# Mixture-of-experts slots: one expert for each slot of 128 pairs, and the last norm's factor put on after the gate product

## The chip, the cores and the metric

The kernel runs on one core of one Trainium2 chip. The metric is the time of one execution on the device, in microseconds (us). Engines are named PE (TensorE, matmul), DVE (VectorE), ACT (ScalarE), POOL (GpSimd) and SP (SyncE, which here only issues transfers).

## The reference, cut to what matters

Two transformer blocks follow each other on 512 tokens of width 1024. The change lies at the end of the first: a mixture of 16 experts in 4 groups, and a gated embedding behind it.

```python
def hierarchical_moe(h, ...):        # top-1 group, then top-2 experts inside it
    a = jnp.einsum('td,edf->tef', ht, w_gate)      # 16 experts, 1024 -> 256
    u = jnp.einsum('td,edf->tef', ht, w_up)
    hid = jax.nn.silu(a) * u * combine[..., None]  # combine is 0 for 14 of 16 experts
    out = jnp.einsum('tef,efd->td', hid, w_down)   # 256 -> 1024

x = x + hierarchical_moe(rms_norm(x, ffn_norm_g), ...)
h3 = rms_norm(x, ple_norm_g)
x = x + jax.nn.sigmoid(h3 @ w_pg) * (p @ w_ple)
```

Only two experts count for a token: 1024 pairs of token and expert.

## The kernel before, in words

**Precision.** Every float32 operand of a large product is split in two float32r parts: ACT copies it (hi), DVE or POOL subtracts (lo), and PE makes three matmuls (hi by hi, lo by hi, hi by lo). For weights this is `split_hi` and `split_lo` (L382, L386); a weight slot is 128 x 2048, 1 MB.

**Routing** (`route_tensor`, `route_scalar`, `route_vector`, L1406 to L1559). DVE finds group and experts with small operations that wait for each other. Tokens are sorted by group into 7 slots of 128 rows (4 groups, 3 spare slots, `SLOTS`). POOL scatters the rows into `sorted_h` in HBM and loads a slot's rows into `hg` (L1641, L1647); the first slot's tokens are permuted by 64 small matmuls (L1437) and are split by ACT (L1789) and DVE (L1833).

**Steps** (`moe_*`, L1601 to L1866). A slot is worked on by all four experts of its group: 28 steps (`STEPS`). A step has three weight units of 1 MB (`unit_in` twice, `unit_down` once), 36 matmuls of 512 columns: 24 for gate and up (`gate_up`, L1729 to L1731), 12 for down (`down`, L1757 to L1759), and two turns of the hidden rows (L1740). Units live in four buffers in turn: SP issues unit u's load once unit u-4 is split (L1608), in order of u; ACT makes hi (L1694) once it has landed and PE has used unit u-4; then DVE makes lo (L1699). `POOL_UNITS` gives the down unit of every second step to POOL. DVE's order in step n is: `hid` (L1848), the down unit's split if it is DVE's, unit 3n+5, `g_lo` (L1853), tokens of the next slot if due, unit 3n+6. PE's order is gate_up(n, 0), turn of hidden n-1, turn of the next slot's tokens (L1711, one step in four), gate_up(n, 1), down(n-1). The four experts add up in PSUM; every fourth step ACT copies the sum to `y_sb` (L1795) and POOL stores it (L1661).

**Behind the steps.** POOL waits for all stores and gathers the rows back into `y_back` (L1675), PE turns them (L1782), DVE adds them to `x` (L1862) and the squares to `ss`, PE sums these (L462), ACT makes `rstd`, DVE and ACT make the normed and split h (L478, L488, L495), and only then does PE begin the gate product with `w_pg`, four slots of 48 matmuls (`ple_*`). The second block's context is turned (L1879) and normed (L1895, L1965 to L1986) between them.

**Other places.** POOL writes zeros over `sorted_h` at the start of the kernel (L1141).

## Time and profile before

| | us |
|---|---|
| median of 3 runs | 1744.39 |
| lowest, highest | 1741.7, 1758.29 |
| the profiled execution | 1744.98 |
| its span | 1743.2 |
| granted clock of the span | 0.985 |

Times in rows are us from the span's start. In a row of the timeline the second number is the length; the bracket holds the idle time before and what ended it. In a group by line the numbers behind the bar are the busy us, the mean ns of one, and the idle time before with what ended it. A row of windows has the length, then the busy us (and count) of PE, PE's weight loads, DVE, ACT and POOL, then the granted clock (1.00 is 2.4 GHz, 0.50 is 1.2 GHz), the busy share of the DMA engines and GB/s.

### The profile page before, as it was taken

To read this page: it belongs to the slowest core of one execution; us is meant where nothing else is said; L and a number is where in the kernel's file an instruction comes from. 1 tells how busy PE (TensorE), PEld (TensorE's weight loads), DVE (VectorE), ACT (ScalarE), POOL (GpSimd) and SP (SyncE) were. 2 spreads that over 40 slices of the span, in tenths; PEclk is the share of its full clock that TensorE was granted. 3 is DMA by queue.
4 is the path that set the end of the run, shared out by engine and by line. 5 is a ranking of instruction groups with operands and counts; after the bars stand their busy time and mean duration, and the time that the engine had idled before them with its cause. 6 is when DMAs were issued, how large, how long until landed. Compare 5 with 4: busy or idle time off the path is not lost.

```text
span 1743.2 us, 20038 instructions
## 1 busy us (share of the span) xinstructions
PE 1655.1 (95%) x7715; PEld 1308.7 (75%) x7715; DVE 875.6 (50%) x1010; ACT 775.9 (45%) x901; POOL 125.0 (7%) x87
## 2 busy tenths in 40 slices
PE   6999999999998889859999999999999999999998
PEld 5777777887876777647688888876788688888886
DVE  6434434444577777747642342421355665565464
ACT  5553454223467666727443343351223543443333
POOL 2101101000222223210010000000000000000000
PEclk8999999999999999979999999999999999999999
DMA  7456553223599999931421211131323133333322
GB/s 226 133 188 222 193 179 123 77 82 125 168 342 346 355 330 323 327 139 49 143 68 49 73 57 64 62 110 49 121 87 105 51 97 105 89 96 98 95 79 67
DMA packets 183202, 247.82 MB, mean 142 GB/s; under 512 B 10236, under 2 KB 151000, under 8 KB 179808
## 3 DMA queue, kind: packets, MB, share of 16 engines
q1 hardware_dynamic: 178911, 232.21, 40.4%
q0 software_dynamic: 4224, 14.72, 2.1%
q8 instruction: 43, 0.70, 0.2%
q14 instruction: 24, 0.19, 0.0%
HBM read 233.23 MB, written 13.67 MB: 142 GB/s over the span
## 4 chain that ended last, share of the span: by engine, by line
PE 78%; DVE 9%; DMA 5%; ACT 4%; issue 2%; SPq 1%; POOL 0%; ACTq 0%; DVEq 0%; POOLq 0%
PE psum L409 20%; PE psum L410 19%; PE psum L411 19%; DMA raw_more<-in_w_up 4%; DVE w_lo_more L1699 3%; PE psum L2466 2%; ACT w_hi_more L1694 1%; PE psum L709 1%; DVE w_lo L1699 1%; DVE pre L488 1%; PE psum L792 1%; PE psum L1203 1%; PE psum L1437 1%; PE psum L1204 1%; PE psum L1205 1%
## 5 line engine op out<-in xcount | busy, mean ns | idle before, releaser
L409 PE MATMUL psum<-h_hi,w_hi 128*128 128x512 f32 x1160 | 466.0, 402 | 7.7 <-DVE w_lo L386 3.2
L411 PE MATMUL psum<-h_hi,w_lo 128*128 128x512 f32 x1160 | 453.5, 391 | 0.0
L410 PE MATMUL psum<-h_lo,w_hi 128*128 128x512 f32 x1160 | 453.4, 391 | 0.0
L386 DVE TENSOR_TENSOR w_lo<-raw,w_hi 128x2048 fp32r<-128x2048 f32 (+2 forms) x99 | 223.7, 2259 | 228.4 <-ACT w_hi L382 228.4
L409 PEld LDWEIGHTS psum<-h_hi,w_hi 128*128 128x128 f32 x1160 | 218.4, 188 | 69.4 <-issue 18.4
L411 PEld LDWEIGHTS psum<-h_hi,w_lo 128*128 128x128 f32 x1160 | 218.6, 188 | 46.9
L410 PEld LDWEIGHTS psum<-h_lo,w_hi 128*128 128x128 f32 x1160 | 218.8, 189 | 46.4 <-issue 3.6
L382 ACT ACTIVATE w_hi<-raw 128x2048 fp32r<-128x2048 f32 (+2 forms) x100 | 187.9, 1879 | 75.3 <-PE psum L411 70.0
L1699 DVE TENSOR_TENSOR w_lo_more<-raw_more,w_hi_more 128x2048 fp32r<-128x2048 f32 x41 | 115.0, 2804 | 50.0 <-ACT w_hi_more L1694 50.0
L439 ACT ACTIVATE sq<-x 128x512 f32<-128x512 f32 x56 | 35.4, 632 | 161.0 <-DVE x L1316 105.2
L1694 ACT ACTIVATE w_hi<-raw 128x2048 fp32r<-128x2048 f32 x42 | 80.4, 1914 | 35.7 <-DMA raw<-in_w_up 16.6
L1694 ACT ACTIVATE w_hi_more<-raw_more 128x2048 fp32r<-128x2048 f32 x41 | 78.5, 1914 | 24.0 <-DMA raw_more<-in_w_up 15.7
L1699 DVE TENSOR_TENSOR w_lo<-raw,w_hi 128x2048 fp32r<-128x2048 f32 x29 | 66.2, 2284 | 20.4 <-ACT w_hi L1694 20.4
L1699 POOL TENSOR_TENSOR w_lo<-raw,w_hi 128x2048 fp32r<-128x2048 f32 x13 | 60.7, 4671 | 146.1 <-ACT w_hi L1694 146.1
L409 PE MATMUL psum<-d_hi,w_hi 128*128 128x512 f32 x176 | 69.3, 394 | 0.0
L410 PE MATMUL psum<-d_lo,w_hi 128*128 128x512 f32 x176 | 69.3, 394 | 0.0
L411 PE MATMUL psum<-d_hi,w_lo 128*128 128x512 f32 x176 | 69.3, 394 | 0.0
L2649 ACT ACTIVATE cv<-psum,vec 128x512 f32<-128x512 f32 x44 | 32.0, 777 | 82.3 <-PE psum L411 82.3
L2672 DVE SCALAR_TENSOR_TENSOR cv<-psum,vec,cv 128x511 f32<-128x511 f32 x44 | 32.8, 746 | 52.7 <-ACT cv L2649 52.7
L1316 DVE SCALAR_TENSOR_TENSOR x<-psum,mod,x 128x512 f32<-128x512 f32 x32 | 23.3, 750 | 51.9 <-PE psum L411 51.9
L1729 PE MATMUL psum<-w_hi_more,s_hi 128*128 128x512 f32 x112 | 45.9, 410 | 1.6 <-DVE s_lo L1833 1.6
L1729 PE MATMUL psum<-w_hi,s_hi 128*128 128x512 f32 x112 | 45.1, 403 | 0.0
(380 smaller groups left out, 2595.4 us busy)
## 6 DMA issues: line engine op xcount, KB each, us to landing
raw<-in_w_up SPq DMA_DIRECT2D x72, 512.0 KB, 6.5
wm_raw<-in_w_mod SPq DMA_DIRECT2D x24, 1024.0 KB, 5.9
raw<-in_w_in SPq DMA_DIRECT2D x18, 1024.0 KB
raw<-in_w_in SPq DMA_DIRECT2D x33, 512.0 KB
raw<-in_w_gate SPq DMA_DIRECT2D x28, 512.0 KB, 5.1
raw_more<-in_w_down SPq DMA_DIRECT2D x28, 512.0 KB, 6.2
raw<-in_w_down SPq DMA_DIRECT2D x28, 512.0 KB, 5.9
raw_more<-in_w_gate SPq DMA_DIRECT2D x27, 512.0 KB, 5.0
```

The costliest lines, as they stand in the source:

```text
L382: act.activation(w_hi[j][:, 0:tiles, :], raw[j][:, 0:tiles, :], ACT.Copy).then_inc(G["hi_ready"], 1)
L386: dve.tensor_tensor(w_lo[j][:, 0:tiles, :], raw[j][:, 0:tiles, :], w_hi[j][:, 0:tiles, :].bitcast(F32), ALU.subtract).then_inc(G["lo_ready ...
L409: pe.matmul(to, w_hi[j][:, tile, :], hi_k, start=(k == 0), stop=False)
L410: pe.matmul(to, w_hi[j][:, tile, :], lo_k, start=False, stop=False)
L411: return pe.matmul(to, w_lo[j][:, tile, :], hi_k, start=False, stop=last)
L439: act.activation(sq[:, c % 2, :], x[:, c, :], ACT.Square).then_inc(G["sq_ready"], 1)
L1694: act.activation(u_hi[b][:, :, :], raw_of(u)[:, :, :], ACT.Copy).then_inc(E["e_whi"], 1)
L1699: eng.tensor_tensor(u_lo[b][:, :, :], raw_of(u)[:, :, :], u_hi[b][:, :, :].bitcast(F32), ALU.subtract)\
L1729: pe.matmul(to, t_hi, hi[:, :, k, :], start=(part == 0 and k == 0), stop=False)
L2466: done = pe.matmul(psum[:, 5 + g % 2, :], fd[:, g, i, part * P:(part + 1) * P], dft_l[:, part, i, :], start=(n == 0), stop=(n == 7))
L2649: act.activation(cv[:, s % 2, half, :], psum[:, 2 * ((j0 + s) % 2) + half, :], ACT.Identity, bias=vec[:, bass.ds(V_CONVB + col, 1)], scale ...
L2672: dve.scalar_tensor_tensor(out=buf[:, 1:T], in0=bank[:, 0:T - 1], scalar=vec[:, bass.ds(V_CONV2 + col, 1)], in1=buf[:, 1:T], op0=ALU.mult, ...
```

## The change: what it does, and the diff

Pairs of token and expert take the place of tokens. There are 16 slots, one for each expert, and 7 spare ones: 23 slots, 23 steps, each with one expert's three units. Each step has its own 128 rows, which POOL gathers from `h_rows` by an indirect DMA two steps ahead; PE turns and ACT and DVE split them in every step. After each step DVE (no longer ACT) copies the 128 x 1024 result and POOL stores it by an indirect DMA to `y_rows`; indices beyond the last row are left out of the transfer. The last slot's result is not stored but spread over the tokens by 16 matmuls with a 0/1 matrix (`last_pick`). `POOL_UNITS` now has the down unit of all steps but the last two. Behind the steps four plain DMAs bring two rows for each token (4 MB), DVE adds the two halves, and the gate product with `w_pg` starts at once on h without the norm's factor; DVE multiplies `rstd` on where the product leaves PSUM. The context's norm moves from behind the second slot to behind the third. The zeros at the start are gone. The routing (not shown in full) works on 16 experts: four operations on 128 x 320, about thirty smaller ones, eight 128 x 128 comparisons (`hot`), and 11 + 9 + 8 small matmuls.

```diff
-RC_U, RC_IOTA, RC_TILE, RC_BEFORE, RC_BLOCK, RC_OWN, RC_HIGH, RC_SLOT = 0, P, P + 4, P + 8, P + 24, P + 40, P + 44, P + 48
-RC_COLS = RC_SLOT + EXTRA * (GROUPS - 1)
+NOWHERE = 4096
+
+
...
+            dve.tensor_tensor(g_exp[:, :, :], rt[:, :, 0:GROUPS], wide(g_top[:, :], GROUPS), ALU.subtract)\
...
+            step(dve.tensor_tensor(in_slot[:, :, :], wide(slots, SLOTS), rows(const_row(RC_SLOT, SLOTS), TOP * NT), ALU.is_equal))
+            codes = rc[:, RC_CODE:RC_LEVEL].rearrange("p (n v o) -> p n v o", v=2, o=1).to_broadcast([P, TOP * NT, 2, SLOTS])
+            dve.tensor_tensor(coded[:, :, :, :], in_slot[:, :, :].rearrange("p n (o s) -> p n o s", o=1)
+                              .to_broadcast([P, TOP * NT, 2, SLOTS]), codes, ALU.mult).then_inc(E["e_hot"], 1)
+            places = place[:, :, :].rearrange("p j i -> p (j i)")
+            for m in range(TOP * NT):
+                dve.tensor_scalar(hot[:, m, :], const_row(RC_PLACE, P), places[:, m:m + 1], None, ALU.is_equal)\
+                   .then_inc(E["e_hot"], 1)
+            dve.wait_ge(E["e_matched"], LISTED)
+            listed = psum[:, ROUTE_BANK, LIST0:LIST0 + 2 * SLOTS]
+            dve.tensor_copy(at_row[:, :, :], listed.rearrange("p (v s) -> p v s", v=2)).then_inc(E["e_routed"], 1)
+            step(dve.tensor_copy(last_row[:, :], listed[:, SLOTS - 1:SLOTS]))
 
...
-        POOL_UNITS = [unit_down(n) for n in range(1, STEPS - 1, 2)]
+        POOL_UNITS = [unit_down(n) for n in range(STEPS - 2)]
...
+            def store_tokens():
+                to = h_rows.rearrange("(i p) d -> p i d", p=P)
+                for half in range(2):
+                    sp.wait_ge(G["h_hi_ready"], 8 * N_MOE + 4 * half + 4)
+                    sp.dma_start(to[:, :, half * T:(half + 1) * T], h_tok[:, :, half * T:(half + 1) * T])\
+                      .then_inc(E["e_stored"], 16)
...
+                if n == 0:
+                    store_tokens()
+                else:
                     load_down(n - 1)
...
+                if n == 4:
+                    sp.wait_ge(E["e_matched"], SHARED)
+                    sp.dma_start(tokens[:, :], const["tokens"]).then_inc(E["e_wr"], 16)
+                if n == 8:
+                    sp.wait_ge(E["e_routed"], LAST_PICKED)
                     sp.dma_start(ctx_in[:, :, :], a["ctx_2"].rearrange("(i p) n -> p i n", p=P)).then_inc(L["ctx_in"], 16)
...
         def moe_gpsimd(pool):
-            pool.wait_ge(W["zero_out"], 16 * (SLOTS + 1))
-            pool.wait_ge(G["h_hi_ready"], 8 * N_MOE + 8)
+            pool.wait_ge(G["chunk_done"], 2 * (G_WO + 3) + 2)
+            for j in range(2):
+                pool.memset(hg[j][:, :], 0.0).then_inc(W["wm_silu"], 1)
+
+            def gather(s):
+                if s >= 2:
+                    pool.wait_ge(E["e_turned"], tokens_turned(s - 2))
+                pool.indirect_dma_start(hg[s % 2][:, :], None, h_rows,
+                                        bass.IndirectOffsetOnAxis(ap=at_row[:, 0, s:s + 1], axis=0),
+                                        bounds_check=T - 1, oob_is_err=False).then_inc(E[f"e_hg{s % 2}"], 16)
+
+            def store_y(s):
+                pool.indirect_dma_start(y_rows, bass.IndirectOffsetOnAxis(ap=at_row[:, 1, s:s + 1], axis=0),
+                                        y_sb[:, :], None, bounds_check=PAIRS - 1, oob_is_err=False)\
...
-                pool.indirect_dma_start(sorted_h, bass.IndirectOffsetOnAxis(ap=at_row[:, i:i + 1], axis=0),
...
-            def load_tokens(s):
-                if s >= 3:
...
+            pool.wait_ge(W["wm_silu"], 5)
+            for s in range(2):
+                gather(s)
+            pool.memset(y_sb[:, :], 0.0).then_inc(W["wm_silu"], 1)
...
+            store_y(SLOTS - 1)
             for n in range(STEPS):
...
+                if n + 2 < SLOTS:
+                    gather(n + 2)
+                if n:
+                    pool.wait_ge(E["e_ycopy"], n)
+                    store_y(n - 1)
                 if unit_down(n) in POOL_UNITS:
                     unit_lo(pool, unit_down(n))
...
+            pool.wait_ge(E["e_ystore"], 16 * SLOTS)
+            wait_unit_lo(pool, UNITS - 1)
             pool.wait_ge(E["e_turned"], tokens_turned(SLOTS - 1))
...
+            from_rows = y_rows.rearrange("(j i p) d -> p j i d", j=TOP, p=P)
+            for half in range(2):
+                for j in range(TOP):
+                    pool.dma_start(y_back[:, j, :, half * T:(half + 1) * T], from_rows[:, j, :, half * T:(half + 1) * T])\
+                        .then_inc(E[f"e_hg{half}"], 16)
...
+        def pick_bank(c):
+            return (6, 7, 0, 1)[c % 4]
+
+        BACK_BANKS, LEAD = (2, 3, 4, 5), 2
...
+            def turn_back(c):
+                if c % 4 == 0:
+                    pe.wait_ge(E["e_chain"], ROUTE_STEPS + KC + c // 4 + 1)
+                if c >= 4:
+                    pe.wait_ge(G["x_ready"], 8 * R_MOE + c - 3)
+                for i in range(NT):
+                    done = pe.transpose(psum[:, BACK_BANKS[c % 4], i * P:(i + 1) * P], y_back[:, 0, i, c * P:(c + 1) * P], ident)
+                done.then_inc(L["turned"], 1)
...
+            def first_gate(c):
+                if c == 0:
+                    pe.wait_ge(G["lo_ready"], G_PG + 1)
+                pe.wait_ge(G["h_lo_ready"], 8 * N_PLE + c + 1)
+                for half in range(2):
+                    done = product(pe, psum[:, half, :], 0, of_pairs(half, c), h_hi, h_lo, c, c == KC - 1)
+                    if c == KC - 1:
+                        done.then_inc(G["chunk_done"], 1)
...
             def down(n):
-                s, e, u = n // PER_GROUP, n % PER_GROUP, unit_down(n)
+                u = unit_down(n)
...
-                if e == 0:
-                    if s:
-                        pe.wait_ge(E["e_ycopy"], s)
-                    else:
-                        pe.wait_ge(L["p_done"], 7)
+                if n:
+                    pe.wait_ge(E["e_ycopy"], n)
+                else:
+                    pe.wait_ge(L["p_done"], 7)
...
+            turn_tokens(0)
+            share()
             for n in range(STEPS):
                 gate_up(n, 0)
                 if n:
                     turn_hidden(n - 1)
-                if n % PER_GROUP == 2 and n // PER_GROUP + 1 < SLOTS:
-                    turn_tokens(n // PER_GROUP + 1)
+                if n + 1 < SLOTS:
+                    turn_tokens(n + 1)
                 gate_up(n, 1)
                 if n:
                     down(n - 1)
...
+            pe.wait_ge(E["e_lo"], LAST)
+            pe.wait_ge(E["e_routed"], LAST_PICKED)
...
+            pe.wait_ge(E["e_chain"], ROUTE_STEPS + KC)
+            for c in range(KC + LEAD):
+                if c < KC:
+                    turn_back(c)
+                if c >= LEAD:
+                    first_gate(c - LEAD)
...
             for n in range(STEPS):
                 act.wait_ge(E["e_used"], unit_in(n, 1) + 1)
...
                 unit_hi(act, 3 * n + 4)
-                if n % PER_GROUP == 0 and n:
-                    copy_y(n // PER_GROUP - 1)
                 unit_hi(act, 3 * n + 5)
...
-                if n % PER_GROUP == 1 and n // PER_GROUP + 1 < SLOTS:
-                    tokens_hi(n // PER_GROUP + 1)
+                if n + 2 < SLOTS:
+                    tokens_hi(n + 2)
                 unit_hi(act, 3 * n + 6)
...
+            def copy_y(n):
+                dve.wait_ge(E["e_used"], unit_down(n) + 1)
+                dve.wait_ge(E["e_ystore"], 16 * n + 16)
+                dve.tensor_copy(y_sb[:, :].rearrange("p (b t) -> p b t", b=2), psum[:, Y_BANK:Y_BANK + 2, :])\
+                   .then_inc(E["e_ycopy"], 1)
+
...
                                          in1=act_u[:, n % 2, :], op0=ALU.mult, op1=ALU.mult).then_inc(E["e_hid"], 1)
                 dve_lo(3 * n + 4)
+                if n:
+                    copy_y(n - 1)
                 dve_lo(3 * n + 5)
                 dve.wait_ge(E["e_hi"], hidden_turned(n))
                 dve.tensor_tensor(g_lo[:, n % 2, :, :], psum[:, HID_BANK + n % 2, 0:2 * P].rearrange("p (j t) -> p j t", j=2),
                                   g_hi[:, n % 2, :, :].bitcast(F32), ALU.subtract).then_inc(E["e_lo"], 1)
-                if e == 1 and s + 1 < SLOTS:
-                    tokens_lo(s + 1)
+                if n + 2 < SLOTS:
+                    tokens_lo(n + 2)
...
+            dve.wait_ge(E["e_hi"], LAST)
...
+            for c in range(KC):
+                dve.wait_ge(E["e_turned"], LAST + c)
+                dve.tensor_tensor(x[:, c, :], x[:, c, :], psum[:, pick_bank(c), :], ALU.add).then_inc(E["e_chain"], 1)
+            for s in range(2):
+                split_lo(dve, G_PG + s, (G_PG + s) % 2)
+            for half in range(2):
+                cols = slice(half * T, (half + 1) * T)
+                dve.wait_ge(E[f"e_hg{half}"], 16 * ((SLOTS + 1 - half) // 2 + TOP))
+                dve.tensor_tensor(y_back[:, 0, :, cols], y_back[:, 0, :, cols], y_back[:, 1, :, cols], ALU.add)\
+                   .then_inc(E["e_chain"], 1)
+            dve.wait_ge(E["e_chain"], ROUTE_STEPS + KC)
...
             for c in range(KC):
                 dve.wait_ge(L["turned"], c + 2)
-                dve.tensor_tensor(x[:, c, :], x[:, c, :], psum[:, c % 4, :], ALU.add).then_inc(G["x_ready"], 1)
+                dve.tensor_tensor(x[:, c, :], x[:, c, :], psum[:, BACK_BANKS[c % 4], :], ALU.add).then_inc(G["x_ready"], 1)
                 if c:
-                    add_square(dve, R_MOE, c - 1, N_MOE + 1)
-            add_square(dve, R_MOE, KC - 1, N_MOE + 1)
+                    gained_lo(c - 1)
+            gained_lo(KC - 1)
+            for c in range(KC):
+                add_square(dve, R_MOE, c, N_MOE + 1)
...
+            for k in range(KC):
+                if k == 4:
+                    norm_mean(pe, N_PLE)
+                    for n in range(2):
+                        turn_context(n)
+                for half in range(2):
+                    done = product(pe, psum[:, 2 + half, :], 1, of_pairs(half, k), h_hi, h_lo, k, k == KC - 1)
+                    if k == KC - 1:
+                        done.then_inc(G["chunk_done"], 1)
             pe.wait_ge(L["ctx_copied"], 2)
             for n in range(2, 4):
...
+                for i in range(2):
+                    c = 2 * s + i
+                    dve.wait_ge(G["chunk_done"], 2 * (G_PG + s) + i + 1)
+                    if c >= 2:
+                        dve.wait_ge(L["pg_sig"], c - 1)
+                    dve.tensor_tensor(pre[:, i, :], psum[:, 2 * ((G_PG + s) % 2) + i, :], rstd[:, :], ALU.mult)\
+                       .then_inc(G["pre_ready"], 1)
...
+                if s == 2:
+                    dve.wait_ge(L["gains"], 3)
+                    context_vector(dve)
```

## Rows read from the trace of the kernel before

**Rows 1.** Windows: the steps, the wait after them, one slot of the gate product.
```profile
505.00:741.00 236.00, 211.18 (x928) 168.95 (x927) 174.61 (x111) 159.84 (x130) 60.86 (x22) 0.98 0.93 339
758.00:773.00 15.00, 0.00 (x0) 0.00 (x0) 2.29 (x1) 2.58 (x2) 4.37 (x5) 0.63 0.64 245
828.90:840.10 11.20, 11.16 (x48) 8.92 (x48) 8.04 (x10) 4.34 (x6) 0.00 (x0) 1.00 0.29 95
```

**Rows 2.** Waits in 505 to 741 us: total, times, longest.
```profile
PEld psum L1757 <- DVE g_lo L1853: 24.4, 13, 4.3
```

**Rows 3.** Chain that ended last, in the steps: start, us, what.
```profile
532.34 1.93 ACT w_hi_more L1694
...
534.29 3.59 DVE w_lo_more L1699
...
538.50 0.41 DVE g_lo L1853
...
545.23 5.89 DMA raw_more<-in_w_up
```

**Rows 4.** Groups by line in 505 to 741 us: busy us, mean ns, idle before.
```profile
L1694 ACT ACTIVATE w_hi_more<-raw_more 128x2048 fp32r<-128x2048 f32 x36 | 68.9, 1915 | 20.7 <-DMA raw_more<-in_w_up 15.7 <-DMA raw_more<-in_w_down 2.9 <-PE psum L1759 2.0
...
L1699 POOL TENSOR_TENSOR w_lo<-raw,w_hi 128x2048 fp32r<-128x2048 f32 x12 | 55.5, 4625 | 140.9 <-ACT w_hi L1694 140.9
L1699 DVE TENSOR_TENSOR w_lo<-raw,w_hi 128x2048 fp32r<-128x2048 f32 x24 | 54.8, 2283 | 16.6 <-ACT w_hi L1694 16.6
...
L1833 DVE TENSOR_TENSOR s_lo<-psum,s_hi 128x1024 fp32r<-128x1024 f32 x5 | 6.0, 1208 | 0.0
```

**Rows 5.** Timeline of POOL and DVE, splits that meet.
```profile
489.06 5.21 POOL L1699 TENSOR_TENSOR w_lo<-raw,w_hi 128x2048 fp32r<-128x2048 f32 x1 [5.26 <-ACT w_hi L1694]
509.71 4.64 POOL L1699 TENSOR_TENSOR w_lo<-raw,w_hi 128x2048 fp32r<-128x2048 f32 x1 [15.44 <-ACT w_hi L1694]
...
489.73 0.48 DVE L1848 SCALAR_TENSOR_TENSOR hid<-psum,comb_s,act_u 128x256 f32<-128x256 f32 x1
...
512.20 4.31 DVE L1699 TENSOR_TENSOR w_lo_more<-raw_more,w_hi_more 128x2048 fp32r<-128x2048 f32 x1 [2.59 <-ACT w_hi_more L1694]
```

**Rows 6.** Timeline of POOL: indirect DMA issues of the routing.
```profile
455.82 2.72 POOL L1641 DMA_INDIRECT sorted_h<-h_tok,at_row  x1 [171.67 <-DVE table L1545]
...
472.18 0.99 POOL L1654 DMA_INDIRECT sorted_comb<-r,at_row  x1 [0.30 <-issue]
473.48 2.03 POOL L1654 DMA_INDIRECT sorted_comb<-r,at_row  x1 [0.30 <-issue]
```

**Rows 7.** Timeline of PE: a down product, the next gate product, a token turn.
```profile
487.72 0.47 PE L1757 MATMUL psum<-w_hi_more,g_hi 128*128 128x512 f32 x1 [2.77 <-DVE g_lo L1853]
...
491.94 0.58 PE L1729 MATMUL psum<-w_hi,s_hi 128*128 128x512 f32 x1
...
495.12 1.06 PE L1711 MATMUL psum<-small,hg 128*128 128x128 f32 x8
```

**Rows 8.** Window of the granted clock within that down product.
```profile
489.00:492.00 3.00, 3.00 (x9) 2.32 (x8) 1.22 (x2) 0.00 (x0) 2.94 (x1) 0.50 0.98 347
```

**Rows 9.** Chain that ended last, from the last down product on.
```profile
757.75 1.03 ACT y_sb L1795
...
759.07 2.91 DMA sorted_y<-y_sb
...
766.57 6.59 DMA y_back<-sorted_y,at_row
```

**Rows 10.** Timeline: routing on DVE, first tokens split, first gate product.
```profile
448.45 0.24 DVE L1502 TENSOR_TENSOR rt<-psum,b_route 128x80 f32<-128x80 f32 x1 [6.03 <-PE psum L1421]
...
454.81 0.17 DVE L1540 CAST at_row<-r 128x4 int32<-128x4 f32 x1
...
469.53 1.02 ACT L1789 ACTIVATE s_hi<-psum 128x1024 fp32r<-128x1024 f32 x1 [14.52 <-PE psum L1437]
...
791.92 0.48 PE L409 MATMUL psum<-h_hi,w_hi 128*128 128x512 f32 x1
```

More of the change, by code:

```diff
@@ L1530, in route_vector @@
-            step(dve.tensor_reduce(tiles, tmp, AX.X, ALU.add))
-            step(dve.tensor_tensor(tmp, rows(tiles), four(RC_BEFORE), ALU.mult))
-            step(dve.tensor_reduce(before, tmp, AX.X, ALU.add))
-            step(dve.tensor_tensor(high, before, rc[:, RC_HIGH:RC_HIGH + 4], ALU.add))
-            step(dve.scalar_tensor_tensor(out=tmp, in0=rank[:, :, :], scalar=float(P), in1=rows(high), op0=ALU.is_ge,
-                                          op1=ALU.mult))
-            step(dve.tensor_tensor(rank[:, :, :], rank[:, :, :], rows(rc[:, RC_OWN:RC_OWN + 4]), ALU.add))
@@ new lines, in route_vector @@
+            for j in range(TOP):
+                step(dve.tensor_tensor(picked[:, j, :, :], choice[:, j, :, :], rows(const_row(RC_OWN, EXPERTS), NT), ALU.mult))
+            step(dve.tensor_reduce(home[:, :, :], picked[:, :, :, :], AX.X, ALU.add))
+            step(dve.memset(extra[:, 0:1], 0.0))
+            dve.wait_ge(E["e_matched"], RANKED)
+            flat_rank = psum[:, ROUTE_BANK, RANK0:RANK0 + NT * EXPERTS]
+            total = psum[:, ROUTE_BANK, RANK0 + NT * EXPERTS:RANK0 + (NT + 1) * EXPERTS]
@@ L1868, in ple_sync @@
+            for c in range(KC):
+                add_square(dve, R_MOE, c, N_MOE + 1)
         def ple_sync(sp):
@@ L1890, in ple_tensor @@
                 turn_context(n)
-            for s in range(4):
-                if s == 1:
+            for s in range(2, 4):
+                if s == 3:
                     pe.wait_ge(L["ctx_sq"], 4)
```

482 lines of the change are left out of this document (252 added, 230 removed).

## The prediction, as made before the changed kernel ran

> **What bounds the kernel now.** I read the page's 40 slices first: PE is busy at nine tenths nearly everywhere, and DMA reaches nine tenths in one stretch only, the expert steps. So the windows of that stretch come next [rows 1]: from 505 to 741 us the DMA engines are busy 0.93 of the time at 339 GB/s, PE shows 211 of 236 us. A step's 36 matmuls need 36 x 0.2325 = 8.4 us (48 take 11.16 us in the last of these rows), and 28 steps take 757.75 - 469.53 = 288.2 us [rows 9, 10], 10.3 each. The table of waits says what PE waits for: `g_lo` of DVE, 13 times, 24.4 us [rows 2]. The chain shows why `g_lo` is late [rows 3]: ACT makes hi of a gate unit, DVE starts its lo at 534.29 and is held for 3.6 us and more, and only at 538.50 comes `g_lo`. The groups by line give the lengths [rows 4]: ACT 1.9 us for a unit, DVE 2.2 to 2.3 when alone, POOL 4.6. The timeline gives the cause [rows 5]: POOL's split runs 509.71 to 514.35; DVE's, begun at 512.20, ends at 516.5, 2.16 us after POOL's, its own length. The other way round, POOL's split of 489.06, begun beside a DVE split, takes 5.21. So a DVE split and a POOL split run one after the other. `hid`, which has one operand in PSUM, takes its usual 0.48 in the middle of a POOL split. Two things thus pace the steps, DMA and the order of splits; both are near 10 us.
>
> **What the change does to a step.** Fewer steps, 23 for 28, but each has more in it. Take the end of a down product as 0.
>
> PE itself: 24 matmuls 5.6, hidden turns 0.2, a token turn in every step 0.85 (eight in 1.06, overlapping the next [rows 7]), 12 down matmuls 2.8: 9.5 us. DMA: weights 3.15 MB as before; 1024 rows of 4 KB gathered and as many stored are 8.4 MB over 23 steps, so 3.51 MB, at 339 GB/s 10.4 us. Neither decides, because of this loop:
> - DVE copies the result out of PSUM: 1024 columns, by `s_lo` 1.2 us [rows 4]. It sat idle before, since the down unit is no longer its own. At 1.2.
> - POOL wakes 0.3 later [rows 9] and issues the store, 1.0 and 0.3 to the next (0.99, then 473.48 after 472.18 [rows 6]). At 2.75 POOL is free.
> - Only now may POOL split the next down unit, because its loop stores first: 4.6.
> - ACT cannot make hi of unit 3n+5 before 0, as its buffer is that of the down unit just used; 1.9, so DVE's split cannot start before 1.95.
> - PE is ready for the next down product at 6.7.
>
> If DVE's unit is late, POOL splits 2.75 to 7.4, DVE 7.4 to 9.6, then `g_lo` (queued behind that split on DVE) to 10.0, down to 12.85. SP issues the next gate unit's load when POOL's split ends, at 7.4 (in order, so the later units queue behind it); 0.4 and 5.9 for the landing [rows 3] make 13.7, which is 0.85 in the next round; hi at 2.8. If DVE then goes first: 2.8 to 5.0, POOL to 9.65, down to 12.55. Either way about 12.7, with DMA no longer full. At the earliest possible hi (1.95) it would be 11.75: the lower end.
>
> **The clock.** In that loop PE stands still some 3 us before every down product. In the trace of before, PE waited some 1.9 us or more before a down product six times; four times the clock was granted at 0.50 (1.2 GHz) within that product, for 3.4 us, once 6.8. The first of them: idle 2.77 before 487.72, the clock 0.50 in 489 to 492, and the next product only at 491.94, so 4.2 for 2.8 [rows 7, 8]. The product is part of the loop. Four of six times 1.4 is 0.9, minus some 0.2 for loads that gain slack: 13.4 us a step. Bounds: 11.75 (nothing of it) and 14.1 (every time).
>
> **The steps' sum.** From the first split of tokens to the end of the first down product: 22.4 before [rows 7, 10]. Added are POOL's split for DVE's (2.3), the second slot's turn and splits in line (0.9 and 1.2): 26.9. Then 20 rounds of 13.4 = 268. The last two down units are DVE's, with no load behind them: 9.5, and 4.0 for turn, hi, lo and down. Sum 308.4 against 288.2: +20.2.
>
> **Routing.** Before, rows are known 6.4 us after the logits (448.45 to 454.81 [rows 10]), with some 30 operations of 0.2. Now three operations on 320 columns before the ranks cost about 0.5 each (estimate: 0.2 and 2.1 us per 2048 columns above it), about 30 of 0.2 to 0.4 follow, and eight comparisons of 0.26: rows are known at about 461. POOL's first indirect issue 2.7 [rows 6], landing 3.5 (by the store at 759.07, 2.9 and its wake-up [rows 9]), turn 1.06: 468.7, where before the 64 matmuls let ACT start at 469.53. I count 0, bounds -2 and +5. The other small matmuls lie in the time in which ACT and DVE split the tokens. Units 2 and 3 queue behind the 2 MB of `h_rows` on SP, but land before 465. The zeros at the start lie beside a full PE: 0, at most -1.
>
> **Behind the steps.** Before, 791.92 - 757.75 = 34.2 us to the first gate product. Now the last store is issued 3 us before the last down product ends and lands at +0.6; POOL then issues four loads of 1 MB. At the rate of the old gather (245 GB/s) 4.2 MB take 17.1 us, at that of the steps (339) 12.4 [rows 1]; I take 15.5, with 0.6 of issue, 2 of fixed time, so +18.5, the third `w_pg` slot being in the same queues. The 16 matmuls, the adds into `x` and two splits (to +12.5) lie within. Then half-add 2.2, `x` 0.7, hi and lo 1.4: first product at +22.8; on DVE the adds of x wait behind both halves, so the first half gains nothing. What was before the slots comes into them: four turns 1.9, the norm sum and first context turns 3.3 and 1.0; a cold clock 1; at the end a multiply by `rstd` 0.7 and a table load behind the moved context 1.2. Sum 31.9: -2.3. Bounds -8 and +3. So most of the head start that the moved factor gives goes into the wait for twice the rows.
>
> **Sum.** 1744.98 (the profiled execution; span 1743.2 and 1.8 around it, 0.6 above the median) + 20.2 + 0 - 2.3 = 1763. Small terms at their middle.
>
> **A rule of the notes beside a row.** One of the two issues made beside DVE splits took 2.03, not 0.99 [rows 6]. The Trainium skill ("SBUF — State Buffer", Who interferes with whom) says that a `tensor_tensor` with both inputs in SBUF takes only the read side of the pair shared with GpSimd, while writing descriptors needs the write side; so an issue beside a split should cost nothing more. By that rule the store's issue stays at 1.0; the row at 473.48 speaks against it.
>
> **Rivals.**
> 1. *Splits pass each other, and DMA paces again (faster).* One mechanism: if POOL's split reads without stopping DVE in the new order, a round is the larger of copy, issue, POOL's split and down (1.2 + 1.55 + 4.65 + 2.85 = 10.3) and DMA 10.4. Then 26.9 + 208 + 13.5 = 248.4, -39.8; with -2.3: 1703. It turns faster than before below about 12.3 a round. Against it: all thirteen meetings go as in [rows 5]. For it: half the DMA time is gone with five steps.
> 2. *The clock holds.* The waits are as said, but the clock stays at 2.4 GHz, as after two of the six waits: 12.6 a round, 16 less: 1747. For it: in 505 to 741 us the mean was 0.98 [rows 1].
> 3. *The store's issue costs 2.0 in each round*, as at 473.48: +1.0 x 20: 1783.
> 4. *The change brings what it counts on*, five steps less at the old 9.9 and nothing else: this would need the loop through the copy, the store and POOL's split not to bind; it ends within rival 1.
>
> **How the numbers follow.** Forecast 0.43, its own range 1750 to 1778; rival 1 0.16, rival 2 0.27, rival 3 0.14. A measurement can tell about 1% (17.4 us). Faster by more: rival 1 and the tail's low bound under rival 2, 0.18. Slower by more (above 1762): rival 3 and two thirds of the forecast, 0.43. Within: 0.39. The range takes in the forecast, rival 2 and most of rival 3, and downwards a tail at its low bound with rounds of 11.75: 1763 - 33 - 6 = 1724, and part of the way to rival 1: 1712 to 1786.
>
> **What would show it.** Down products 12.5 to 14 us apart, with PE idle about 3 us before each, ended by `g_lo` or POOL's `w_lo`; POOL's splits starting within 2 us of each copy of y; DVE splits of 3 to 6.8 us; DMA share below 0.8 in the steps; clock 0.50 in many windows. The first product with `w_pg` 20 to 26 us after the last down product. Rounds under 11.5 us would prove the loop wrong; rounds of 12.5 with the clock at 1.00 would make rival 2 right; issues of 2 us rival 3.

## The result, and the profile after

The changed kernel takes 1791.79 us (median of 4 runs, 1787.95 to 1795.03) beside 1749.45 for the kernel before in the same session: a ratio of 1.0255, 95% interval 1.0217 to 1.0292. Forecast were 1763 and a range of 1712 to 1786: slower was right, the size was not, and the time lies outside the range. The profiled execution took 1795.03 with a span of 1793.2, so 50.0 us more span than before.

The page of the changed kernel: the granted clock in 40 slices, the head of the chain, and four groups (busy us, mean ns, idle before).

```profile
PEclk9999999999589888889899999999999999999999
...
PE psum L442 19%; PE psum L443 19%; PE psum L444 19%; DMA hg<-h_rows,at_row 3%; POOL w_lo_more L1755 2%; PE psum L2614 2%; PE psum L742 1%; PE psum L824 1%; DMA raw_more<-in_w_up 1%; DVE w_lo L1755 1%; DVE w_lo_more L1755 1%; POOL y_rows L1705 1%; PE psum L1229 1%; PE psum L1230 1%; PE psum L1231 1%
...
L1755 DVE TENSOR_TENSOR w_lo_more<-raw_more,w_hi_more 128x2048 fp32r<-128x2048 f32 x23 | 91.0, 3957 | 26.0 <-ACT w_hi_more L1750 26.0
...
L1795 PE MATMUL psum<-small,hg 128*128 128x128 f32 x184 | 32.2, 331 | 40.2 <-DMA hg<-h_rows,at_row 40.2
...
L1700 POOL DMA_INDIRECT hg<-h_rows,at_row x23 | 62.3, 2710 | 45.7 <-issue 41.5
...
L1755 POOL TENSOR_TENSOR w_lo_more<-raw_more,w_hi_more 128x2048 fp32r<-128x2048 f32 x11 | 57.2, 5202 | 13.8 <-ACT w_hi_more L1750 13.6
```

Two rows have no counterpart before. PE's token turn (L1795) waits 40.2 us for the DMA that gathers its rows, and that gather heads the chain behind the matmuls. And an issue of a gather (L1700) takes POOL 2.7 us, not 1.0. DVE's splits of this buffer take 3.96 us in the mean instead of their own 2.3: many of them are held by POOL's.

The same stretch of the steps as in [rows 1], in windows (PE, PEld, DVE, ACT and POOL busy, clock, DMA share, GB/s), and the waits from the first down product to the 21st (509 to 791 us; total, times, longest):

```profile
505.00:741.00 236.00, 185.05 (x763) 149.54 (x763) 169.81 (x101) 117.63 (x98) 150.62 (x50) 0.88 0.75 261
```

```profile
POOL y_rows L1705 <- DVE y_sb L1936: 97.7, 20, 8.8
...
PE psum L1795 <- DMA hg<-h_rows,at_row: 31.5, 12, 5.0
...
PE psum L1846 <- POOL w_lo_more L1755: 16.4, 7, 3.3
...
PE psum L1846 <- POOL w_lo L1755: 7.3, 3, 2.5
PE psum L1846 <- DVE g_lo L1956: 3.6, 1, 3.6
```

DMA falls from 0.93 to 0.75, as forecast (below 0.8); the clock from 0.98 to 0.88. PE waits before the down product, released by POOL's unit, as forecast, but 31.5 us of waits stand somewhere else, before the token turn.

The timeline of two rounds (start, us, what, idle before), POOL first, then DVE, then the token turn between them:

```profile
524.27 1.00 POOL L1705 DMA_INDIRECT y_rows<-y_sb,at_row  x1 [3.73 <-DVE y_sb L1936]
525.29 4.54 POOL L1755 TENSOR_TENSOR w_lo_more<-raw_more,w_hi_more 128x2048 fp32r<-128x2048 f32 x1
530.00 2.90 POOL L1700 DMA_INDIRECT hg<-h_rows,at_row  x1 [0.16 <-issue]
537.99 3.08 POOL L1705 DMA_INDIRECT y_rows<-y_sb,at_row  x1 [5.08 <-DVE y_sb L1936]
541.10 4.59 POOL L1755 TENSOR_TENSOR w_lo<-raw,w_hi 128x2048 fp32r<-128x2048 f32 x1
545.85 2.91 POOL L1700 DMA_INDIRECT hg<-h_rows,at_row  x1 [0.16 <-issue]
```

```profile
522.24 1.22 DVE L1936 COPY y_sb<-psum 128x1024 f32<-128x1024 f32 x1 [2.22 <-PE psum L1848]
526.24 5.75 DVE L1755 TENSOR_TENSOR w_lo<-raw,w_hi 128x2048 fp32r<-128x2048 f32 x1 [2.78 <-ACT w_hi L1750]
531.92 0.41 DVE L1956 TENSOR_TENSOR g_lo<-psum,g_hi 128x256 fp32r<-128x256 f32 x1
...
537.90 2.29 DVE L1755 TENSOR_TENSOR w_lo_more<-raw_more,w_hi_more 128x2048 fp32r<-128x2048 f32 x1 [0.71 <-ACT w_hi_more L1750]
```

```profile
527.54 1.16 PE L1795 MATMUL psum<-small,hg 128*128 128x128 f32 x8 [2.35 <-DMA hg<-h_rows,at_row]
```

Read from the down product that ends at 522.20: copy of y until 523.46, POOL wakes at 524.27, store, split to 529.83, DVE's split to 531.99, `g_lo` to 532.33, and the down product ends at 535.85, 13.65 later. That is the loop that I had written down. New is the third POOL row: the gather for the next but one slot stands behind the split.

A round is the time from the end of one down product to the end of the next. The 20 rounds from 508.63 to 791.04 take 282.4 us, 14.12 each. They are of two kinds that mostly alternate: eleven wait 1.6 to 3.6 us before the down product, and in eight of these it then takes 4.4 to 5.5 us instead of 3.0, with the clock at 0.50 within it; the other nine wait 2.2 to 5.0 us before the token turn, and the clock is at 0.50 in their gate product.

Where the 50.0 us come from, in the two traces:

| stretch | before | after | more | forecast |
|---|---|---|---|---|
| start to first router turn | 437.94 | 439.59 | +1.7 | 0 |
| router turns and products, to the last | 10.4 | 16.2 | +5.8 | 0 |
| logits to first hi of the tokens | 21.2 | 24.9 | +3.7 | 0 |
| first block | 22.6 | 27.9 | +5.3 | +4.5 |
| to the end of the last down product | 265.6 | 296.0 | +30.4 | +15.7 |
| last down to first `w_pg` product | 34.2 | 19.1 | -15.1 | -11.4 |
| from there to the next stage's slot | 58.0 | 74.5 | +16.5 | +9.1 |
| rest | 893.3 | 894.9 | +1.6 | 0 |

The beginning of the steps: the clock window of the router, the logits and the rows known on DVE, the first hi on ACT, in that order.

```profile
443.00:455.00 12.00, 12.00 (x64) 12.00 (x63) 1.08 (x2) 4.98 (x10) 0.00 (x0) 0.52 0.24 89
```

```profile
455.90 0.24 DVE L1518 TENSOR_TENSOR rt<-psum,b_route 128x80 f32<-128x80 f32 x1 [11.82 <-PE psum L1447]
...
470.01 0.21 DVE L1583 CAST at_row<-psum 128x46 int32<-128x46 f32 x1 [0.85 <-PE psum L1467]
...
480.72 1.02 ACT L1888 ACTIVATE s_hi<-psum 128x1024 fp32r<-128x1024 f32 x1 [12.05 <-PE psum L1795]
```

The router's products, which the change does not touch, run at 1.2 GHz here; before they ran at 2.4.

### The profile page after: what moved, and what is told of

Read it like the earlier page. It is cut to its first block, busy times and chain, and to the rows that moved or that the text cites. A ratio compares the mean times of both kernels' runs of the same rounds, so it can differ in the third digit from the quotient of the medians.

```text
span 1793.2 us, 19900 instructions
## 1 busy us (share of the span) xinstructions
PE 1662.1 (93%) x7643; PEld 1316.6 (73%) x7643; DVE 915.6 (51%) x1027; ACT 753.5 (42%) x886; POOL 237.5 (13%) x114
## 4 chain that ended last, share of the span: by engine, by line
PE 76%; DVE 7%; DMA 5%; ACT 4%; POOL 4%; issue 2%; SPq 1%; POOLq 0%; ACTq 0%; DVEq 0%
PE psum L442 19%; PE psum L443 19%; PE psum L444 19%; DMA hg<-h_rows,at_row 3%; POOL w_lo_more L1755 2%; PE psum L2614 2%; PE psum L742 1%; PE psum L824 1%; DMA raw_more<-in_w_up 1%; DVE w_lo L1755 1%; DVE w_lo_more L1755 1%; POOL y_rows L1705 1%; PE psum L1229 1%; PE psum L1230 1%; PE psum L1231 1%
## 5 line engine op out<-in xcount | busy, mean ns | idle before, releaser
L1755 DVE TENSOR_TENSOR w_lo_more<-raw_more,w_hi_more 128x2048 fp32r<-128x2048 f32 x23 | 91.0, 3957 | 26.0 <-ACT w_hi_more L1750 26.0
L1750 ACT ACTIVATE w_hi_more<-raw_more 128x2048 fp32r<-128x2048 f32 x34 | 64.9, 1910 | 54.0 <-DMA raw_more<-in_w_up 38.6
L1755 DVE TENSOR_TENSOR w_lo<-raw,w_hi 128x2048 fp32r<-128x2048 f32 x24 | 73.2, 3049 | 20.5 <-ACT w_hi L1750 20.5
L1750 ACT ACTIVATE w_hi<-raw 128x2048 fp32r<-128x2048 f32 x34 | 64.9, 1909 | 26.6 <-DMA raw<-in_w_up 20.2
L1795 PE MATMUL psum<-small,hg 128*128 128x128 f32 x184 | 32.2, 331 | 40.2 <-DMA hg<-h_rows,at_row 40.2
L1700 POOL DMA_INDIRECT hg<-h_rows,at_row x23 | 62.3, 2710 | 45.7 <-issue 41.5
L1755 POOL TENSOR_TENSOR w_lo_more<-raw_more,w_hi_more 128x2048 fp32r<-128x2048 f32 x11 | 57.2, 5202 | 13.8 <-ACT w_hi_more L1750 13.6
L1795 PEld LDWEIGHTS psum<-small,hg 128*128 128x128 f32 x184 | 27.1, 203 | 42.8 <-DMA hg<-h_rows,at_row 42.6
```

The lines of the kernel that those rows point to most:

```text
L1700: pool.indirect_dma_start(hg[s % 2][:, :], None, h_rows, bass.IndirectOffsetOnAxis(ap=at_row[:, 0, s:s + 1], axis=0), bounds_check=T - 1, ...
L1750: act.activation(u_hi[b][:, :, :], raw_of(u)[:, :, :], ACT.Copy).then_inc(E["e_whi"], 1)
L1755: eng.tensor_tensor(u_lo[b][:, :, :], raw_of(u)[:, :, :], u_hi[b][:, :, :].bitcast(F32), ALU.subtract)\
L1795: done = pe.transpose(psum[:, b + k // 4, (k % 4) * P:(k % 4 + 1) * P], of_k[:, k, :], ident)
```

## The experiments

Theory, after the traces: the round is the loop I had, plus a clock that halves in nearly every round, plus the gather behind POOL's split. Rivals: the scattered rows are slow whatever POOL does; DMA's limit; only the splits count, and not what stands ahead of them. Behind each time stands its ratio to the kernel before with the 95% interval. Rounds, waits and windows are of the one profiled execution of each run.

**All splits on DVE**, in the changed kernel and in the kernel before:

```
-        POOL_UNITS = [unit_down(n) for n in range(STEPS - 2)]
+        POOL_UNITS = []
```

> The changed kernel with every weight split on DVE; POOL only issues gathers and stores. Theory A (a POOL split and a DVE split exclude each other, POOL's split stands behind copy and store, and the gather's issue behind the split takes 2.9 us): without POOL's splits a round is DVE's own work, 3 x 2.2 + 1.2 + 1.2 + 0.5 + 0.4 = 9.9 us, or DMA's 10.4; rounds of 10.0 to 10.8 us, gather issues of 1.0 us unless they start beside a running split, no waits for the gather, clock near 1.00: 282.4 us for 20 rounds become 200 to 216, in all 1710 to 1728. Theory B (the scattered rows themselves are slow, 6 to 8 us to landing, and the token turn waits for them whatever POOL does): waits before the token turn stay, rounds above 12.5 us, 1760 or more. Theory C (DVE, now with all splits, becomes the bound with its waits): rounds of 11.5 to 12.5, 1740 to 1760.

> The kernel before with every weight split on DVE. DVE then has 7.6 us of work in a step and DMA, at 0.93, 9.6 to 10.3. If the exclusion of the splits cost the kernel before only its 13 waits for g_lo (24.4 us), at most that comes back and DMA paces the rest: 1730 to 1745. If the exclusion were hidden behind DMA there: 1745 to 1750. Beside the run of the changed kernel with the same edit it says what the change itself is worth once POOL splits nothing.

Measured: 1722.68 us for the changed kernel (ratio to before 0.9839, 0.9798 to 0.9880) and 1724.97 for the kernel before (0.986, 0.9821 to 0.9899). Windows of both, the changed kernel first:

```profile
505.00:715.00 210.00, 188.33 (x866) 155.10 (x865) 183.74 (x135) 136.16 (x114) 60.53 (x37) 0.95 0.90 325
```

```profile
505.00:715.00 210.00, 205.65 (x921) 166.41 (x919) 178.68 (x121) 157.56 (x127) 4.84 (x9) 0.99 0.99 374
```

Taking POOL's splits away is worth 69 us to the changed kernel (in the traces 60.6 of it in the 20 rounds; the two executions also differ in the router's clock, see the last section) and some 23 to the one before. Without them the two are level: the whole change, five steps less with twice the rows moved, wins nothing. In the changed kernel 20 rounds take 221.8 us, 11.1 each, a little over the 10.8 I gave, since 10 of them still wait for a gather. In the kernel before, DMA is now at 0.99, and what comes back is nearly the whole of the 24.4 us that [rows 2] has. I had given it 1730 to 1745: I had expected DMA to keep more of it, but its rate rose from 339 [rows 1] to 374 GB/s.

Its trace also shows what an issue does beside a split: POOL and DVE, same stretch.

```profile
662.53 2.29 POOL L1705 DMA_INDIRECT y_rows<-y_sb,at_row  x1 [6.80 <-DVE y_sb L1936]
665.12 1.02 POOL L1700 DMA_INDIRECT hg<-h_rows,at_row  x1 [0.30 <-issue]
```

```profile
661.65 2.28 DVE L1755 TENSOR_TENSOR w_lo_more<-raw_more,w_hi_more 128x2048 fp32r<-128x2048 f32 x1
...
665.71 2.29 DVE L1755 TENSOR_TENSOR w_lo<-raw,w_hi 128x2048 fp32r<-128x2048 f32 x1 [0.31 <-ACT w_hi L1750]
```

The issue at 662.53 falls into a split that ends at 663.93, and ends 0.89 after it; the one at 665.12 begins ahead of a split and takes 1.02. In the changed kernel the gather of 530.00 ends 0.91 after DVE's split, the store of 537.99 0.88 after it.

**A third gather buffer**: the gather stays at its place in POOL's loop, one round further ahead (the buffer itself and its semaphore are left out of the cut).

```
-                if n + 2 < SLOTS:
-                    gather(n + 2)
+                if n + 3 < SLOTS:
+                    gather(n + 3)
```

> The changed kernel with a third gather buffer: each gather is issued at the same place of POOL's loop, but one round further ahead. Theory A: every second round waits 2.2 to 5.0 us for its gather before the token turn; these waits vanish, the rounds become like the others (12.0 with the clock held, 13.5 with it halved in the down product), mean 12.8 to 13.4, so 14 to 26 us less: 1766 to 1778. Theory B (the loop of splits paces both kinds of rounds, the wait for the gather lies beside it): the wait only moves to the down product, mean 13.7 to 14.1: 1783 to 1792.

Measured: 1795.57 (1.0247, 1.0210 to 1.0284). Theory B, 3.6 above its range. Its waits in 509 to 791 us and its window:

```profile
PE psum L1846 <- DVE g_lo L1956: 38.1, 10, 5.9
...
PE psum L1846 <- POOL w_lo L1755: 20.3, 9, 2.3
```

```profile
505.00:741.00 236.00, 185.76 (x748) 148.27 (x747) 166.75 (x100) 115.91 (x97) 142.41 (x48) 0.85 0.73 257
```

No token turn waits any more, and nothing is won: every round now waits before its down product, and the 20 rounds take 289.7 us. The clock is now halved in 18 of the 20 down products (4.3 to 5.5 us) where it was in eight. So the wait for the gather lay beside the loop of splits. My first reading of the long rounds, that the gather made them, fell here.

**POOL splits before it stores**:

```
+                if unit_down(n) in POOL_UNITS:
+                    unit_lo(pool, unit_down(n))
                 if n:
                     pool.wait_ge(E["e_ycopy"], n)
                     store_y(n - 1)
-                if unit_down(n) in POOL_UNITS:
-                    unit_lo(pool, unit_down(n))
```

> The changed kernel with POOL splitting its unit before it waits for the copy of y and issues the store. Theory A (my loop: copy, wake-up, store issue, then split, 3.1 us before the split starts): the split starts when ACT's hi is there, 1 to 2 us after the down product, and the down product 1 to 2 us earlier: rounds of 11 to 12.8 us, 1740 to 1768. Theory D (only the sum of the two engines' splits counts, not what stands ahead of POOL's): rounds stay at 13.5 to 14.1, 1780 to 1792.

Measured: 1749.79 (1.0022, 0.9989 to 1.0055), 42 us less, as theory A says. Its POOL and its waits in 509 to 740 us:

```profile
548.43 4.62 POOL L1755 TENSOR_TENSOR w_lo<-raw,w_hi 128x2048 fp32r<-128x2048 f32 x1 [5.66 <-ACT w_hi L1750]
553.22 2.87 POOL L1705 DMA_INDIRECT y_rows<-y_sb,at_row  x1 [0.17 <-issue]
```

```profile
PE psum L1795 <- DMA hg<-h_rows,at_row: 27.0, 8, 4.3
```

POOL now splits while the down product ends (548.92) and stores behind that. The 20 rounds take 240.4 us, 42.0 less than 282.4. Eight of them fall to 9.4 to 9.8 us, three take 10.3 to 10.4, and nine 11.9 to 16.6, eight of them with a wait of 2.2 to 4.3 for the gather. The copy, the wake-up and the issue ahead of the split, 3.1 us in each round, do set the loop.

**Both remedies with the third buffer**: first all splits on DVE, then the split ahead of the store.

> The changed kernel with both edits, every split on DVE and a third gather buffer. With the splits on DVE alone, 10 of 20 rounds took 9.5 to 9.8 us and the others 10.0 to 16.4, each with a wait for the gather before the token turn but for one. Theory A (the gathers' landing is all that is left over DVE's 9.9 us): no wait before a token turn, 20 rounds in 195 to 208 us instead of 221.8 (one round still long, at the wait for a load), in all 1696 to 1712, faster than the kernel before by 2 to 3%. Theory B (these waits only show DMA's limit; the rows come earlier and the weights later): 1715 to 1725.

> The changed kernel with POOL's split ahead of the store and a third gather buffer. With the split ahead alone rounds alternated between 9.75 us and 12 to 16.5, the long ones with 2.2 to 4.3 us of wait for the gather before the token turn. Theory A: this wait goes and the long rounds fall to 10 to 12: 20 rounds in 198 to 220 instead of 240.4, in all 1707 to 1730. Theory B (what the gather's wait hid is the exclusion of the splits, at 12.7 us a round): 250 us, 1745 to 1760, as with the third buffer alone, which gained nothing.

Measured: 1722.56 (0.9863, 0.9809 to 0.9918) and 1731.23 (0.9929, 0.9904 to 0.9954), the second just above theory A's range. No token turn waits. The first in 600 to 690 us: its window, some of its waits, and one copy of y with the store ahead of it:

```profile
600.00:690.00 90.00, 80.83 (x383) 65.08 (x382) 81.66 (x60) 62.38 (x51) 29.70 (x18) 1.00 0.91 334
```

```profile
DVE y_sb L1936 <- DMA y_rows<-y_sb,at_row: 8.3, 8, 1.5
...
ACT w_hi_more L1750 <- DMA raw_more<-in_w_down: 1.8, 2, 0.9
```

```profile
632.71 2.28 POOL L1705 DMA_INDIRECT y_rows<-y_sb,at_row  x1 [7.01 <-DVE y_sb L1936]
...
641.09 1.23 DVE L1936 COPY y_sb<-psum 128x1024 f32<-128x1024 f32 x1 [0.73 <-DMA y_rows<-y_sb,at_row]
```

The 20 rounds take 216.0 us instead of 221.8. The time is in theory B's range, but the trace names another cause than DMA's limit. Weights are hardly waited for: in this window ACT waits 4.9 us in all for their landing. What comes back in every round is DVE's wait for the store of y before: there is one `y_sb`, and DVE may copy into it only when the last store has landed. Copy 1.2, POOL's waking 0.8, an issue of 2.3 that is held by DVE's own split, and 6.1 to 6.9 to the landing make 10.4 to 11.3, which is the round; 14 of the 20 wait so, 14.8 us together. In the last rounds, where DVE waits for nothing, a round is 9.6, DVE's own work. That DMA, busy 0.91, makes the landing as long as it is may be; no run here has a second `y_sb`, so the share of each is open.

The profiled execution took 1726.95, against 1721.61 of the run without the third buffer: in it the clock was halved in the router (last section) and the first down product ended 8.2 us later, which is more than the rounds gave back. Whether this also holds the medians level is not shown. With the split ahead of the store the third buffer takes the ratio from 1.0022 to 0.9929, some 16 us, and the rounds from 240.4 to 222.4: there the gather's wait did decide (and DVE then waits for the store of y in 17 of the 20 rounds). What a wait is worth depends on what stands behind it.

**The clock**: the third buffer and three matmuls ahead of each down product, into a bank that nobody reads then.

```
                 if n:
+                    if n >= 2:
+                        fill(n - 1, 3)
                     down(n - 1)
```

> The changed kernel with the third gather buffer and three extra matmuls (some 2.0 us at full clock, into the gate bank that nobody reads then) ahead of each down product, in the 2.3 to 3.7 us in which PE waits there. With the third buffer alone the 20 rounds took 289.7 us, 14.5 each, and the down products 4.3 to 5.5 us in 18 of them instead of 2.97. Theory A (14.5 is 12.65 of the loop of splits and 1.8 of the halved clock): down products of 3.0 us, rounds alternately 12.0 and 13.3, 253 to 262 us, so 28 to 36 less than 1795: 1759 to 1768. Theory B (the halved clock lies beside waits that would take the time anyway, or it is halved despite the matmuls): 1785 to 1797.

Measured: 1780.75 (1.0211, 1.0141 to 1.0281), between the two theories. These are two executions, and their interval overlaps that of the third buffer alone, so what follows is read from one trace each. Its window:

```profile
505.00:741.00 236.00, 206.84 (x897) 158.65 (x895) 182.46 (x104) 126.23 (x105) 155.45 (x53) 0.97 0.76 264
```

The clock rises from 0.85 to 0.97, 17 of 20 down products take 3.0 us, and the rounds 270.6 us instead of 289.7, 0.96 less each. The down products together are 27.6 us shorter, so 0.4 a round of what the clock costs there was slack, or went to the extra matmuls. Without the three rounds in which the clock fell all the same, the mean is 13.0: this is the loop itself.

**The tail.** After the fourth `w_pg` slot the changed kernel's PE stands still; waits in 876 to 892 us:

```profile
PE psum L442 <- DVE pre L2094: 9.9, 1, 9.9
```

In the first edit DVE's context work is put behind the two multiplications for which PE waits (`context_vector` called after them in the last slot instead of at the end of the third); in the second the norm is formed as in the kernel before (its `ple_*` functions, with the sum over `x` ahead of the first product), the slots of pairs staying as they are.

> The changed kernel with the context norm's work on DVE put behind the last two multiplications by rstd (for which PE waits 9.9 us at 876 to 886) instead of ahead of them. From the end of the fourth gate slot to the first product of the next stage's slot it is 21.9 us in the changed kernel and 9.8 in the kernel before. Theory A (DVE's sum of work there is the bound: the multiplications by rstd, the context's 16 operations, the adds and the squares): PE's wait moves to before the norm's sum, these 21.9 us stay 20 to 22.5, in all 1789 to 1795. Theory B (the order is what costs): 13 to 17 us, in all 1783 to 1787.

> The changed kernel with one of its two parts undone: the last norm is formed as in the kernel before (sum, rstd, then hi and lo of the normed x, sigmoid straight from PSUM, the context's norm at its old place), the slots of pairs stay. In the changed kernel the stage from the first w_pg product to the first product of the next stage's slot takes 74.5 us (823.78 to 898.29), in the kernel before 58.0. Theory A (what the moved factor wins, the norm's 18.7 us ahead of the first product, it gives back as DVE's multiplications by rstd, the turns between the products and PE's wait of 9.9 us): the first product comes at 819.4 + 18.7 = 838, the next slot at 896: 1786 to 1793, no difference. Theory B (the moved factor wins on balance): 1797 to 1806. Theory C (it loses on balance by more than 5 us): under 1785.

Measured: 1801.79 for one execution of the first, and 1788.75 (1.0258, 1.0224 to 1.0293) for the second. PE's waits in the first, 875 to 910 us:

```profile
PE psum L495 <- DVE ss L483: 6.0, 1, 6.0
PE psum L442 <- DVE hc_lo L2134: 2.8, 2, 2.6
```

From the fourth slot's end (883.80) to the next slot (906.66) it is 22.9 us, against 21.9: the wait moves to the norm's sum, as theory A says (though 22.9 and the time both lie above its ranges). But that DVE's sum of work is the bound does not follow. DVE is busy 14.2 of the 22.9 us and ACT 13.9, and only DVE's order was changed:

```profile
881.74 0.68 DVE L2094 TENSOR_TENSOR pre<-psum,rstd 128x512 f32<-128x512 f32 x1
...
891.92 1.28 ACT L2067 ACT_TABLE_LOAD   x1
893.22 0.63 ACT L2067 ACTIVATE sig<-pre 128x512 f32<-128x512 f32 x1
```

The first half of the slot is ready for its sigmoid at 882.4, but ACT still has the context's eight operations, each of which waits for DVE, and a table load ahead of it, until 893.22. An order that puts them behind the sigmoids on ACT too was not run, so theory B is not excluded. Of the 6.7 us that its span is longer than the changed kernel's, 6.0 had come by the last down product (810.63 against 804.67), ahead of the edit. The old norm has its first product at 835.03 and the next slot at 892.98, so 91.2 us after the last down product against 93.6 with the moved factor, and the times agree within their intervals: moving the factor wins nothing.

**Towards a faster kernel.** First the old norm on top of the two edits; then instead of it the context's megabyte, which SP loads in the ninth round, loaded behind the last weights; then all four.

> All splits on DVE, third gather buffer, and the old norm. By theory A of the old norm's run it equals the run with the two edits alone, 1715 to 1725; if the moved factor wins, 1728 or more.

> All splits on DVE, third gather buffer, and the context's 1 MB, which SP loads in the ninth round behind a wait, loaded behind the last weights. With the two edits alone one round took 17.4 us against 10.5 around it, with ACT waiting 9.5 us for a gate unit's load behind that megabyte. If that load is the reason, the round falls to 10.5 and nothing comes back at the end, where DMA is free: 7 us less, 1712 to 1718. If DMA's limit gives it back elsewhere: 1719 to 1725.

> The changed kernel with four edits together: every split on DVE, third gather buffer, the context's megabyte behind the last weights, and the old norm. The profiles put the old norm's stage at 91.2 us from the last down product to the next stage's slot (801.81 to 892.98) against 93.6 with the moved factor (804.67 to 898.29), so some 2.4 less than the three edits' 1715.7: 1711 to 1716. If the old norm is worth nothing beside the others: 1714 to 1719.

Measured: 1718.48 (0.9858, 0.9823 to 0.9893), 1715.74 (0.984, 0.9818 to 0.9862) and 1711.4 (0.9795, 0.9767 to 0.9823). The long round of 17.4 us is 10.72 with the late load. The single steps are not resolved: even the interval of all four edits overlaps that of all splits on DVE alone (0.9798 to 0.9880). Clear is the distance to the two kernels: 2% under the kernel before, 4.5% under the changed one. In 505 to 690 us DVE again waits for the store of y, 16.9 us in 16 rounds; no run takes that away. The window of the steps with all four edits:

```profile
505.00:690.00 185.00, 167.67 (x797) 135.51 (x797) 168.09 (x123) 127.42 (x104) 56.24 (x35) 1.00 0.93 334
```

## Why the prediction was right in its sign and wrong in its size

*The order of splits is the bound, and rounds exclude rival 1.* Right. The loop is there link by link, DMA is no longer full (0.75). Rival 1 had rounds of 10.4 at DMA's pace with POOL's splits; without them they are 10.8 to 11.1, and there DVE waits for the store of y, so that they come so near to 10.4 does not show DMA's pace.

*12.7 a round without the clock.* Nearly right: 13.0, as far as the run with the extra matmuls shows it. One term that was too short is POOL's waking: 0.3 was taken from [rows 9], but the store starts 0.8 after the copy's end, and POOL is free at 3.1 and not 2.75. That the token turn would come at once was wrong too (the gather's issue was left out of the loop, at 2.9 us behind the split), but it cost nothing in this kernel, as the third buffer shows.

*The clock, +0.9 - 0.2.* This step is too low. Four of six waits before were taken as the share. After, the clock falls in 17 of 20 rounds, in the kind that waits for the gather within the gate product, in the other within the down product. The nearest measure is 0.96 net, from the third buffer alone to the same with the extra matmuls (18 halved down products against 3); in the changed kernel itself no run holds the clock. That the upper bound, 14.1 every time, is so near the 14.12 that came is luck: two other terms are in the 14.12.

*One round's load.* Missing. The context's megabyte, with the wait ahead of it on SP, lengthens one round (17.1 us in the changed kernel; moved away, it gave the 20 rounds back 5.1 us, 210.9 for 216.0). I had not priced SP's extra load in the ninth round. The three together, 0.3, 0.26 and up to 0.25 a round, each from another run, are about the step of 0.72 from 13.4 to the 14.12 measured: 14.4 us of the 32 that are missing (1795.03 against 1763). The other large parts are the routing, 11.2, and the tail, 5.3.

*The last two down products* (13.5, measured 13.6) and *the first block* (26.9, measured 27.9): right.

*Routing 0, -2 to +5.* This step failed by the most for its size. Of its 11.2 us 1.7 had come before the router and 5.8 are the halved clock in the router's own products, which [rows 10] show nothing of. The rest is 3.7: the rows are known 14.1 us after the logits and not 12.5, as DVE waited 2.5 for PE's ranks, which ran at the halved clock; and from there to the first hi it takes 10.5 instead of 7.7, with 5.0 from the first issue's end to the turn for the 3.5 taken from the store, and a turn of 1.97 at 1.2 GHz (0.8 of it was in hand, as the forecast's 468.7 lay that much under 469.53). With the clock held in the router, as in the run of all splits on DVE, the first turn is at 470.49 and not at 478.71. Over all executions with the changed routing, ACT's first hi comes at 470.24 to 473.80 where the clock was held, within the forecast's bounds, and at 480.35 to 480.74 where it was halved. So what failed is in the main the clock in the router and behind it, put at nothing.

*Tail -2.3.* Its first half was better than forecast (19.1 for 22.8 us to the first product): the last rows landed 13.4 us after the last down product and not 18.5, and what decided was DVE, busy without a break from 807.8 with the adds, two splits and from 817.0 the half-adds. The second was worse: what comes into the slots was priced at 9.1 us, with DVE's eight multiplications at 0.7 for the last one and the moved context at a table load. It measured +16.5: PE waits 9.9 for the last multiplications, which stand behind the context's 16 operations on DVE; these take 7.7 and begin 2.9 late, behind two table loads on ACT. With the rest, +3.0 for -2.3.

*Rival 2*, that the clock holds, is excluded; *rival 3*, a store of 2.0 us, is right in kind but hits three stores of 20, which took 2.9 to 3.1; the others began at most 0.02 us into one of DVE's splits, or beside none, and took 1.0. It is the gathers, behind POOL's own split, that nearly all hit. The row at 473.48 [rows 6] had told this rightly, against the rule beside it.

Three sums of the prediction are off by 0.1 to 0.4: the terms of the first block add up to 26.8 and not 26.9, those of the rows' landing behind the steps to 18.7 and not 18.5, those up to the first turn to 468.3 and not 468.7. None of them matters beside the terms above.

## What to carry to other kernels

When one engine splits and also issues transfers, write its loop out in full, every issue with what it waits for, and price each issue by whether it falls into the other engine's split. A step that makes PE stand still 2 to 4 us in each round cost the clock in 17 of 20 rounds here: do not carry over the share seen when waits were rare (four of six). And take a wait away in a copy of the kernel before blaming it: the gather's 31.5 us were worth nothing until the split had been moved, and some 16 after. And when a time comes out as a theory said, still ask the trace what is waited for: here it was a store that had to leave the one buffer, and how much of that is DMA's rate is open.

## What the runs showed of the hardware

- An indirect DMA issue on POOL that falls into a running `tensor_tensor` split of DVE ends after that split: 0.88 to 0.91 us in the rows shown, 0.8 to 1.1 in every such issue of all executions, so it takes up to 3.1 us. One that begins ahead of the split, or up to 0.03 us into it, takes 1.0. A plain issue (`dma_start`) does not wait: in the kernel before and in the same with all splits on DVE, the 17 loads and stores of token rows that begin inside such a split take 0.53 to 0.59 us, as they do beside none (0.56). One of them, with its split:

```profile
569.19 0.53 POOL L1647 DMA_DIRECT2D hg<-sorted_h  x1 [11.02 <-PE psum L1711]
...
568.75 2.29 DVE L1699 TENSOR_TENSOR w_lo_more<-raw_more,w_hi_more 128x2048 fp32r<-128x2048 f32 x1 [0.86 <-ACT w_hi_more L1694]
```

  The Trainium skill ("SBUF — State Buffer", Who interferes with whom) lets only POOL's reads wait for such a split, and infers that descriptor writing, which needs the other side, does not. The plain issues agree with it; the measurement decides against using it for an indirect issue. A plain issue has no list of rows to read, so it may be this reading that waits; that is not shown.
- The granted clock in the router's products, 1.2 or 2.4 GHz, differs from one execution to the next with the same instructions ahead of it. Of the 12 profiled executions that have the changed routing it was halved in seven (0.50 to 0.62 in 440 to 455 us) and held in five (0.89 to 1.00); it was held in both that have the old routing. It moves the first down product by some 8 us. Whether the change has a part in it stays open.
